# Turning queries, keys, convolution inputs and attention probabilities without TensorE

## The chip, the core and the metric

The kernel runs on one core of a Trainium2 chip. The metric is the device time of one execution in microseconds, the median of several runs. TensorE (PE in the rows) does the matrix products, VectorE (DVE) and ScalarE (ACT) the elementwise work, SyncE (SP) does nothing but issue DMA transfers, and GpSimd (POOL) has a few constants and row loads. Each engine works through its own list of instructions in order; semaphores tie the lists together.

## What is computed

Three blocks over 256 tokens of width 2048, in fp32 throughout: a gated MLP block, a stick-breaking attention block of 16 heads, and a block with an mLSTM branch (4 heads of 256) and a softmax attention branch (8 heads of 128), followed by an MLP. The parts that the change touches:

```python
# stick-breaking attention, per block of 128 queries
z = jnp.einsum('bhqd,bhkd->bhqk', qblk, kh)
a = jnp.where(mask, jnp.exp(log_sigmoid(z) + tail), 0.0)
o = jnp.einsum('bhqk,bhkd->bhqd', a, vh)

# mLSTM queries and keys: causal depthwise convolution of width 4, then silu
up = jnp.pad(u, ((0, 0), (3, 0), (0, 0)))
out = b
for j in range(4):
    out = out + w[j] * up[:, j:j + S]

# softmax attention (one block of 256 keys), after rotary embedding
p = jax.nn.softmax(jnp.where(causal, q @ k.T * scale, -inf))
o = p @ v
```

A matrix product contracts over the partition axis. So queries and keys, which the projections give with tokens on the partitions, have to be turned to have the head's channels there, the probabilities have to be turned to have the keys there, and the convolution wants channels on the partitions and tokens along the free axis.

## The kernel before

Weights stream from memory once. They are cut into 914 **groups** of 512 KB. A group is loaded by one DMA into one of 5 slots of `t_stage` (`load_group`), then split by ScalarE into a high part `t_wh` (`split_group`, an ACTIVATE of 128x1024) and by VectorE into the rest `t_wl` (a TENSOR_TENSOR of 128x1024). TensorE then runs 12 matmuls of 128x512 on it in `proj`: low weights by high input, high by high, high by low, for two 128-row tiles of weights and two halves of the tokens. `AHEAD = 4`: before the matmuls of group j the split of group j+4 is written out, and that split may start only when TensorE has finished group j-1, since there are 5 slots of split weights too. `load_group` waits for the split that frees its slot of `t_stage`.

Everything else is cut into **pieces**, which `later()` puts into one first-in, first-out list. After each group `offer()` may write out the next piece, if it has waited its number of groups (1 unless stated). So a piece's instructions stand on every engine between two groups, and their place in each engine's order is fixed when the program is built. `t_pool4` is a ring of four 4 KB-a-partition buffers (`temps`), `trans` two PSUM banks for transposes, `misc` two for small products.

What the change touches, before:

- `heads_t` (L906) turns a chunk of four heads of queries or keys in two pieces. Each takes 4 TensorE transposes against the identity (a **set** below) into a PSUM bank, and one ScalarE copy to `qt`, `kt_` in `t_vreg`. It is called 8 times in the stick-breaking block and 4 times in the softmax branch.
- `turn` (L949) turns a 128x512 tile of probabilities by one set and one ScalarE copy; three units in each of 4 chunks of the stick-breaking block and of 2 chunks of the softmax branch. In the stick-breaking block `four` calls it and `five` uses its result in `weighted`; in the softmax branch `two` and `three` do.
- `conv_t` (L1210) turns two heads of 128 channels at a time by a set, ScalarE copies them into `pad` behind three zero columns, `taps` computes the 4 taps per head on VectorE, and `second` the silu. Four calls.
- `to_xt` (L552) is another way to turn, in use already for the inputs of the large products: VectorE transposes 32x32 blocks within their partitions (two STREAM_TRANSPOSE of 128x512), then four DMAs on SyncE's queue, one per quarter of the partitions, carry the blocks to their place. The reader waits for the four landings. At most four such transfers are under way (`s_turn`).

Of the kernel before, what the change touches and what calls it, by code (L numbers as in the profile page):

```python
# [179 lines left out]
def _program(nc, A, out, ctx):  # L180
# [30 lines left out]
    pad, _ = sb("pad", [128, 2, 260], offset=s_at + 4096)  # L211
# [339 lines left out]

    def to_xt(src, marks, c, xh, xl, ready, gain=None, scale=1.0, done=None, wait=1):  # L552
# [3 lines left out]
        def send():  # L556
            zn, z, free = temps.take()
            quadrants = xl[:, 4 * c:4 * c + 4, :].bitcast(F32).rearrange("p k (i a s) -> p a (k i) s", i=2, a=4)
            zv = z.rearrange("p x y -> p (x y)")
            blocks = zv.rearrange("p (b k i s) -> p b k i s", b=4, k=4, i=2)  # L560
            for i in range(2):
                turned = DV.do(lambda e, i=i: e.block_transpose(
                    blocks[:, :, :, i], src(i).rearrange("p (k r b) -> p b k r", k=4, b=4)), *marks, *free)
            if done is not None:
                done(turned)
            n = turn_count[0]
            turn_count[0] += 1
            s_ = s_turn[n % 4]
            before = ((s_, 64 * (n // 4)),) if n >= 4 else ()
            for a in range(4):  # L570
                landed = SP.dma(lambda e, a=a: e.dma_start(
                    quadrants[:, a], zv[32 * a:32 * a + 32, :]),
                    s_, 64 * (n // 4) + 64, turned, *before)
            temps.give(zn, landed)
            st["landed"] = landed
# [337 lines left out]
    def heads_t(src, mark, dst, marks, done, wait=1):  # L913

        for b in range(2):
            def piece(b=b):
                x, m = src(), mark()
                n, t, free = trans.take()
                for j in range(2):
                    for i in range(2):  # L920
                        f = lambda e, j=j, i=i: e.transpose(t[:, 256 * j + 128 * i:256 * j + 128 * i + 128],
                                                            x[:, i, 128 * (2 * b + j):128 * (2 * b + j) + 128],
                                                            ident)
                        if i == 1 and j == 1:
                            tp = PE.do(f)
                        else:
                            PE.run(f, m, *free)
                a = AC.do(lambda e: e.activation(dst[:, 2 * b:2 * b + 2, :], t.rearrange("p (h s) -> p h s", h=2),
                                                 ACT.Copy), tp)
                trans.give(n, a)  # L930
                marks.append(a)
                if b == 1:
                    done(tp)
            later((piece, wait if b == 0 else 1))

    def scores(q, k, i, heads, marks):

        nk = 128 * (i + 1)
        n, t, free = misc.take()
        for j, h in enumerate(heads):  # L940
            f = lambda e, j=j, h=h: e.matmul(t[:, nk * j:nk * j + nk], q[:, h, 128 * i:128 * i + 128],
                                             k[:, h, 0:nk], start=True, stop=True)
            if j == len(heads) - 1:
                mm = PE.do(f)
            else:
                PE.run(f, *marks, *free)
        return n, t.rearrange("p (h k) -> p h k", k=nk), mm

    def turn(src, dst, mark):  # L949

        n, t, free = trans.take()
        for b in range(4):
            f = lambda e, b=b: e.transpose(t[:, 128 * b:128 * b + 128], src[:, 128 * b:128 * b + 128], ident)
            if b == 3:
                tp = PE.do(f)
            else:
                PE.run(f, mark, *free)
        a = AC.do(lambda e: e.activation(dst, t, ACT.Copy), tp)
        trans.give(n, a)
        return a  # L960
# [17 lines left out]
    def sb_unit(c, i, heads, qk_marks, v_view, v_mark, finish):  # L978
# [33 lines left out]
        def five():  # L1012
            n, t, mm = weighted(st["r"], v_view, i, heads, st["a"], v_mark)
# [193 lines left out]
    pad_free = [()]  # L1207
    pad_mark = DV.do(lambda e: e.memset(pad[:, :, 0:3], 0.0), *h_marks[3])

    def conv_t(src, mark, dst, base, marks, done):  # L1210

        def taps(j, b, s):
            ch = base + 2 * b + j
            x = s["t"][:, 0, 256 * j:256 * j + 256]
            m = DV.do(lambda e: e.tensor_scalar(x, pad[:, j, 0:256], cw[:, ch:ch + 1], gc[:, 80 + ch:81 + ch],
                                                ALU.mult, ALU.add), s["a"], *s["free"])
            for w in range(1, 4):
# [5 lines left out]
        for b in range(2):  # L1223
            s = {}

            def first(b=b, s=s):
                n, t, free = trans.take()
                for j in range(2):
                    for i in range(2):
                        f = lambda e, j=j, i=i: e.transpose(t[:, 256 * j + 128 * i:256 * j + 128 * i + 128],  # L1230
                                                            src[:, i, 128 * (2 * b + j):128 * (2 * b + j) + 128],
                                                            ident)
                        if i == 1 and j == 1:
                            tp = PE.do(f)
                        else:
                            PE.run(f, mark, *free)
                a = AC.do(lambda e: e.activation(pad[:, :, 3:259], t.rearrange("p (h s) -> p h s", h=2), ACT.Copy),
                          tp, pad_mark, *pad_free[0])
                trans.give(n, a)
                s["n"], s["t"], s["free"] = temps.take()  # L1240
                s["a"] = a
                taps(0, b, s)
                if b == 1:
                    done(tp)

            def second(b=b, s=s):
                m = taps(1, b, s)
                x, th = s["t"][:, 0, :], s["t"][:, 1, :]
                pad_free[0] = (m,)
# [5 lines left out]
            later((first, 2), second)  # L1255
# [207 lines left out]
    def soft_unit(c, u, i, heads, q, k, v, qk_marks, v_mark, ha, finish):  # L1463
# [25 lines left out]
        def three():  # L1489
            n, t, mm = weighted(st["r"], v, i, heads, st["t"], v_mark)  # L1490
# [12 lines left out]
    def soft_chunk(c):  # L1503
# [32 lines left out]
        later(u0[0], u1[0], u0[1], u0[2], u1[1], u2[0], u1[2], (u2[1], 2), u2[2])  # L1536
# [243 lines left out]
```

How the kernel before makes its waits and increments, by code:

```python
    def wait(self, *marks):  # L87
        for sem, value in marks:
            if self.seen.get(sem.name, 0) < value:
                self.seen[sem.name] = value
                self.items.append(lambda e, s=sem, v=value: e.wait_ge(s, v))
# [1 line left out]
    def do(self, emit, *marks):  # L93
        self.wait(*marks)
        self.n += 1
        f = emit(BOUND)
        self.items.append(lambda e: f(e).then_inc(self.sem, 1))
        return (self.sem, self.n)
# [5 lines left out]
    def dma(self, emit, sem, value, *marks):  # L105
        self.wait(*marks)
        f = emit(BOUND)
        self.items.append(lambda e: f(e).then_inc(sem, 16))
        return (sem, value)
```

## Time and profile before

| | us |
|---|---|
| median of 3 runs (2634.42 to 2636.94) | 2636.9 |
| the profiled execution, its own time | 2635.97 |
| its span in the profile | 2634.2 |
| TensorE busy | 2614.1 (99%) |
| VectorE busy | 1603.1 (61%) |
| ScalarE busy | 1218.5 (46%) |
| chain that ended last | TensorE 95% |

TensorE has hardly any idle time. Its matmuls are pipelined: one of 128x512 has a duration of about 390 ns in the rows, but the next starts 227 ns later, so cost is read from starts and not from durations. The blocks in time: gated MLP up to about 756 us, stick-breaking attention to about 1115, its output product to about 1205, the mLSTM projections and gates to about 1465, the softmax branch to about 1610, and then products to the end.

### The profile page before, as it was taken

To read this page: it belongs to the slowest core of one execution; us is meant where nothing else is said; L and a number is where in the kernel's file an instruction comes from. 1 tells how busy PE (TensorE), PEld (TensorE's weight loads), DVE (VectorE), ACT (ScalarE), POOL (GpSimd) and SP (SyncE) were. 2 spreads that over 40 slices of the span, in tenths; PEclk is the share of its full clock that TensorE was granted. 3 is DMA by queue.
4 is the path that set the end of the run, shared out by engine and by line. 5 is a ranking of instruction groups with operands and counts; after the bars stand their busy time and mean duration, and the time that the engine had idled before them with its cause. 6 is when DMAs were issued, how large, how long until landed. Compare 5 with 4: busy or idle time off the path is not lost.

```text
span 2634.2 us, 29949 instructions
## 1 busy us (share of the span) xinstructions
PE 2614.1 (99%) x11775; PEld 2162.1 (82%) x11775; DVE 1603.1 (61%) x1852; ACT 1218.5 (46%) x1478; POOL 20.8 (1%) x46
## 2 busy tenths in 40 slices
PE   9999999999999999999999999999999999999999
PEld 7888888888888888887888888888878888888887
DVE  5546665566657666766866666555576565565564
ACT  6554443444454444455444444444454344344443
POOL 1000000000000000000000000000000000000000
PEclk9999999999999999999999999999999999999999
DMA  7666666676765555677565666666657566676773
GB/s 250 192 193 202 204 197 201 193 211 197 216 203 173 171 166 167 191 226 222 160 179 173 183 185 184 200 200 200 219 172 224 192 204 214 189 217 207 199 223 130
DMA packets 437997, 515.39 MB, mean 196 GB/s; under 512 B 198480, under 2 KB 200640, under 8 KB 437856
## 3 DMA queue, kind: packets, MB, share of 16 engines
q1 hardware_dynamic: 435328, 506.29, 63.4%
q0 software_dynamic: 2384, 6.93, 1.1%
q8 instruction: 92, 1.51, 0.2%
q14 instruction: 49, 0.40, 0.0%
q10 hardware_dynamic: 144, 0.26, 0.0%
HBM read 488.24 MB, written 2.10 MB: 186 GB/s over the span
## 4 chain that ended last, share of the span: by engine, by line
PE 95%; DVE 2%; DMA 1%; ACT 1%; issue 1%; SPq 1%; DVEq 0%; ACTq 0%
PE bank L33 94%; PE bank L36 1%; DVE t_wl L51 1%; SPq L72 1%; DMA t_ytl<-t_pool 0%; DMA t_stage<-in_a_w_in_dram 0%; ACT t_wh L42 0%; DVE t_pool L39 0%; DVE t_pool L51 0%; ACT t_pool L42 0%; ACT t_yth L42 0%; DMA t_xtl<-t_pool 0%; ACT t_xth L42 0%; DVE t_pool L54 0%; DVE t_hres L51 0%
## 5 line engine op out<-in xcount | busy, mean ns | idle before, releaser
L51 DVE TENSOR_TENSOR t_wl<-t_stage,t_wh 128x1024 fp32r<-128x1024 f32 x914 | 1101.9, 1220 | 686.1 <-ACT t_wh L42 684.3
L42 ACT ACTIVATE t_wh<-t_stage 128x1024 fp32r<-128x1024 f32 x914 | 953.2, 1056 | 823.2 <-PE bank L33 809.5
L33 PE MATMUL bank<-t_wl,t_xth 128*128 128x512 f32 x2496 | 987.0, 395 | 9.4 <-DVE t_wl L51 7.0
L33 PE MATMUL bank<-t_wh,t_xtl 128*128 128x512 f32 x2496 | 973.8, 390 | 0.0
L33 PE MATMUL bank<-t_wh,t_xth 128*128 128x512 f32 x2496 | 972.4, 390 | 0.2 <-ACT t_wh L42 0.2
L33 PEld LDWEIGHTS bank<-t_wl,t_xth 128*128 128x128 f32 x2496 | 469.4, 188 | 106.5 <-DVE t_wl L51 9.3
L33 PEld LDWEIGHTS bank<-t_wh,t_xtl 128*128 128x128 f32 x2496 | 469.1, 188 | 99.8 <-DVE t_wl L51 0.5
L33 PEld LDWEIGHTS bank<-t_wh,t_xth 128*128 128x128 f32 x2496 | 469.6, 188 | 95.1 <-ACT t_wh L42 0.6
L33 PE MATMUL bank<-t_wl,t_yth 128*128 128x512 f32 x1024 | 399.2, 390 | 0.0
L33 PE MATMUL bank<-t_wh,t_ytl 128*128 128x512 f32 x1024 | 398.4, 389 | 0.0
L33 PE MATMUL bank<-t_wh,t_yth 128*128 128x512 f32 x1024 | 398.3, 389 | 0.0
L33 PEld LDWEIGHTS bank<-t_wl,t_yth 128*128 128x128 f32 x1024 | 192.2, 188 | 40.4 <-DVE t_ytl L54 0.3
L33 PEld LDWEIGHTS bank<-t_wh,t_yth 128*128 128x128 f32 x1024 | 192.2, 188 | 40.1 <-issue 0.2
L33 PEld LDWEIGHTS bank<-t_wh,t_ytl 128*128 128x128 f32 x1024 | 192.2, 188 | 39.8
L54 DVE SCALAR_TENSOR_TENSOR t_ytl<-t_ytl,t_yth 128x1024 fp32r<-128x1024 f32 x32 | 39.2, 1225 | 127.8 <-ACT t_yth L42 127.8
L42 ACT ACTIVATE t_pool<-bank,t_scl 128x512 f32<-128x512 f32 x120 | 75.9, 684 | 82.2 <-PE bank L33 77.0
L42 ACT ACTIVATE t_yth<-t_ytl 128x1024 fp32r<-128x1024 f32 x32 | 33.9, 1061 | 147.0 <-DMA t_ytl<-t_pool 147.0
L39 DVE STREAM_TRANSPOSE t_pool<-t_pool 128x512 f32<-128x512 f32 x72 | 74.2, 1069 | 0.0
L51 DVE TENSOR_TENSOR t_pool<-t_pool 128x1024 f32<-128x1024 f32 (+2 forms) x48 | 39.3, 819 | 25.1 <-ACT t_pool L42 23.3
L42 ACT ACTIVATE t_vreg<-bank 128x512 f32<-128x512 f32 (+1 forms) x39 | 21.6, 555 | 69.4 <-PE bank L36 42.2
L33 PE MATMUL bank<-t_wl,t_mth 128*128 128x512 f32 x128 | 49.8, 389 | 0.0
L33 PE MATMUL bank<-t_wh,t_mth 128*128 128x512 f32 x128 | 49.8, 389 | 0.0
(195 smaller groups left out, 978.6 us busy)
## 6 DMA issues: line engine op xcount, KB each, us to landing
t_stage<-in_a_w_in_dram SPq DMA_DIRECT2D x192, 512.0 KB, 4.4
t_stage<-in_w_in_dram SPq DMA_DIRECT2D x178, 512.0 KB, 4.2
t_stage<-in_b_w_in_dram SPq DMA_DIRECT2D x128, 512.0 KB, 3.7
t_stage<-in_w_up_dram SPq DMA_DIRECT2D x128, 512.0 KB, 3.9
t_stage<-in_w_down_dram SPq DMA_DIRECT2D x128, 512.0 KB, 4.2
t_stage<-in_a_w_out_dram SPq DMA_DIRECT2D x64, 512.0 KB, 4.2
t_ytl<-t_pool SPq DMA_DIRECT2D x128, 128.0 KB, 3.2
t_stage<-in_b_w_out_dram SPq DMA_DIRECT2D x32, 512.0 KB, 5.3
```

Of the source, the lines that this page charges most:

```text
L33: return lambda e: e.matmul(*a, **k)
L36: return lambda e: e.transpose(*a, **k)
L39: return lambda e: e.transpose(out, in_)
L42: return lambda e: e.activation(*a, **k)
L51: return lambda e: e.tensor_tensor(*a, **k)
L54: return lambda e: e.scalar_tensor_tensor(*a, **k)
L72: return lambda e: e.dma_start(*a, **k)
```

## The change

`send_turned` and `turn_chunk` are the two halves of `to_xt`, made functions of their own. `heads_t` becomes one piece: two STREAM_TRANSPOSE and four DMAs into the query or key buffer; it takes one more buffer of the ring, and its DMAs wait also for the last scores that read the buffer. `turn` becomes one STREAM_TRANSPOSE of 128x512 from `e` to `r` and four DMAs of half the bytes back into `e`. `conv_t` turns all four heads at once in a piece `send`, into a second ring buffer, and computes the taps two groups later from there; a tap that looks back by n tokens reads and writes ranges shifted by n, so `pad` and its zeros are gone. In `soft_chunk` the second unit's turn now stands before the first unit's weighted sum, and the last weighted sum waits two groups.

```diff
     def heads_t(src, mark, dst, marks, done, wait=1):
-        for b in range(2):
-            def piece(b=b):
...
-                a = AC.do(lambda e: e.activation(dst[:, 2 * b:2 * b + 2, :], t.rearrange("p (h s) -> p h s", h=2),
-                                                 ACT.Copy), tp)
...
-            later((piece, wait if b == 0 else 1))
+        def piece():
+            x = src()
+            n, z, free = temps.take()
+            zv = z.rearrange("p x y -> p (x y)")
+            turned = turn_chunk(lambda i: x[:, i, :], zv, (mark(), *free))
+            done(turned)
+            landed = send_turned(zv, dst.rearrange("p h (i a s) -> p a (h i) s", i=2, a=4), turned, *scored)
+            temps.give(n, landed)
+            marks.append(landed)
+        later((piece, wait))
...
+    def turn(src, via, mark):
+        turned = DV.do(lambda e: e.block_transpose(
+            via.rearrange("p (b c s) -> p b c s", b=4, c=4), src.rearrange("p (c r b) -> p b c r", c=4, b=4)), mark)
+        return send_turned(via, src.rearrange("p (c a s) -> p a c s", c=4, a=4), turned)
...
+    def send_turned(flat, rows, turned, *marks):
+        n = turn_count[0]
+        turn_count[0] += 1
+        s_ = s_turn[n % 4]
+        before = ((s_, 64 * (n // 4)),) if n >= 4 else ()
+        for a in range(4):
+            landed = SP.dma(lambda e, a=a: e.dma_start(rows[:, a], flat[32 * a:32 * a + 32, :]),
+                            s_, 64 * (n // 4) + 64, turned, *before, *marks)
+        return landed
...
-                m = DV.do(lambda e: e.scalar_tensor_tensor(
-                    out=x, in0=pad[:, j, w:w + 256], scalar=cw[:, 16 * w + ch:16 * w + ch + 1], in1=x,
-                    op0=ALU.mult, op1=ALU.add), m)
+                m = DV.do(lambda e: e.scalar_tensor_tensor(
+                    out=y[:, back:256], in0=x[:, 0:256 - back],
+                    scalar=cw[:, 48 - 16 * back + ch:49 - 16 * back + ch], in1=y[:, back:256],
+                    op0=ALU.mult, op1=ALU.add), m)
...
+        later((send, 2), (f0, 2), s0, f1, s1_)
...
-        later(u0[0], u1[0], u0[1], u0[2], u1[1], u2[0], u1[2], (u2[1], 2), u2[2])
+        later(u0[0], u1[0], u0[1], u1[1], u0[2], u2[0], u1[2], (u2[1], 2), (u2[2], 2))
```

The change moves instructions on the queues. Three places, each before and after. First, SyncE's list through the first chunk and a half of the stick-breaking block (`t_stage<-in_b_w_in_dram` is a weight load, `t_pool_61` the ring, `t_vreg` the query or key buffer).

```order
L72 DMA t_stage<-in_b_w_in_dram 128x2x512 [waits dve] x113
```

```order
L72 DMA t_stage<-in_b_w_in_dram 128x2x512 [waits dve] x12
L72 DMA t_pool_61<-t_pool_61 128x4x32 [waits turn2,dve]
L72 DMA t_pool_61<-t_pool_61 128x4x32 x3
L72 DMA t_stage<-in_b_w_in_dram 128x2x512 [waits dve] x5
L72 DMA t_pool_61<-t_pool_61 128x4x32 [waits turn3,dve]
L72 DMA t_pool_61<-t_pool_61 128x4x32 x3
L72 DMA t_stage<-in_b_w_in_dram 128x2x512 [waits dve] x5
```

Where only weights were loaded, each unit now puts four small transfers between two loads; twelve weight loads after the keys comes the first, and five loads lie between the units.

Second, VectorE's list at the first convolution (`t_gsm`, `t_dt`: the gates' last piece; `t_cw`: tap weights).

```order
L51 TENSOR_TENSOR t_dt<-t_dt,t_tri 128x1024 [waits act]
L51 TENSOR_TENSOR t_wl<-t_stage,t_wh 128x1024 [waits pe,act] x2
L48 TENSOR_SCALAR t_pool_61<-t_pad,t_cw,t_gc 128x256 [waits dve,act]
L54 SCALAR_TENSOR_TENSOR t_pool_61<-t_pad,t_cw,t_pool_61 128x256 [waits dve] x3
L51 TENSOR_TENSOR t_wl<-t_stage,t_wh 128x1024 [waits pe,act]
L48 TENSOR_SCALAR t_pool_61<-t_pad,t_cw,t_gc 128x256
```

```order
L51 TENSOR_TENSOR t_dt<-t_dt,t_tri 128x1024 [waits act]
L51 TENSOR_TENSOR t_wl<-t_stage,t_wh 128x1024 [waits pe,act] x2
L39 STREAM_TRANSPOSE t_pool_61<-t_pool_61 128x16x32 [waits dve]
L39 STREAM_TRANSPOSE t_pool_61<-t_pool_61 128x16x32
L51 TENSOR_TENSOR t_wl<-t_stage,t_wh 128x1024 [waits pe,act] x2
L48 TENSOR_SCALAR t_pool_61<-t_pool_61,t_cw,t_gc 128x256 [waits turn0]
```

The first tap waited for a ScalarE copy; now it waits for the transfer (`turn0`), two splits after the transposes. The four pieces of taps then follow in four consecutive groups, where they had three groups for two.

Third, VectorE's list in the softmax branch, from the end of the keys' rotary embedding to the first unit's mask (`t_neg`).

```order
L51 TENSOR_TENSOR t_pool_61<-t_pool_61 128x4x64 [waits dve]
L51 TENSOR_TENSOR t_wl<-t_stage,t_wh 128x1024 [waits pe,act] x5
L51 TENSOR_TENSOR t_pool_61<-bank,t_neg 128x512 [waits dve,pool,pe]
```

```order
L51 TENSOR_TENSOR t_pool_61<-t_pool_61 128x4x64 [waits dve]
L51 TENSOR_TENSOR t_wl<-t_stage,t_wh 128x1024 [waits pe,act] x3
L39 STREAM_TRANSPOSE t_pool_61<-t_pool_61 128x16x32 [waits dve]
L39 STREAM_TRANSPOSE t_pool_61<-t_pool_61 128x16x32
L51 TENSOR_TENSOR t_wl<-t_stage,t_wh 128x1024 [waits pe,act]
L51 TENSOR_TENSOR t_pool_61<-bank,t_neg 128x512 [waits turn2,pool,pe]
```

The keys' transposes stand one split ahead of the first unit, so on TensorE one group of matmuls lies between that place and the scores that read the keys.

## Rows read from the trace of the kernel before

**Rows 1.** The page: busy time of each engine.
```profile
PE 2614.1 (99%) x11775; PEld 2162.1 (82%) x11775; DVE 1603.1 (61%) x1852; ACT 1218.5 (46%) x1478; POOL 20.8 (1%) x46
```
**Rows 2.** Groups by line: count, busy us, mean ns, idle before and releaser.
```profile
L36 PE MATMUL bank<-t_ident,t_pool 128*128 128x128 f32 x200 | 29.9, 272 | 1.5 <-DVE t_pool L51 1.5
```
**Rows 3.** TensorE's timeline (start us, us) at the first queries, stick-breaking block.
```profile
753.71 0.39 PE L33 MATMUL bank<-t_wl,t_xth 128*128 128x512 f32 x1
...
756.44 0.60 PE L36 MATMUL bank<-t_ident,t_pool 128*128 128x128 f32 x4
...
759.65 0.60 PE L36 MATMUL bank<-t_ident,t_pool 128*128 128x128 f32 x4
```
**Rows 4.** Critical chain at two turns by DMA; the DMA issues of a small load.
```profile
1078.38 1.06 DVE t_pool L39
...
1082.35 3.21 DMA t_ytl<-t_pool
...
1088.95 2.08 DVE t_pool L39 x2
...
1093.23 3.11 DMA t_ytl<-t_pool
```
```profile
t_vreg<-in_norm_g_dram SPq DMA_DIRECT2D x1, 16.0 KB, 1.6
```
**Rows 5.** VectorE's and TensorE's timelines at stick-breaking units: split, then weighted sum.
```profile
815.16 1.22 DVE L51 TENSOR_TENSOR t_wl<-t_stage,t_wh 128x1024 fp32r<-128x1024 f32 x1
...
829.63 1.22 DVE L51 TENSOR_TENSOR t_wl<-t_stage,t_wh 128x1024 fp32r<-128x1024 f32 x1
...
1054.34 2.35 DVE L51 TENSOR_TENSOR t_wl<-t_stage,t_wh 128x1024 fp32r<-128x1024 f32 x2
...
1066.47 1.22 DVE L51 TENSOR_TENSOR t_wl<-t_stage,t_wh 128x1024 fp32r<-128x1024 f32 x1 [0.17 <-ACT t_wh L42]
```
```profile
820.52 1.05 PE L33 MATMUL bank<-t_vreg,t_pool 128*128 128x128 f32 x8
...
836.41 1.05 PE L33 MATMUL bank<-t_vreg,t_pool 128*128 128x128 f32 x8
...
1058.77 1.05 PE L33 MATMUL bank<-t_vreg,t_pool 128*128 128x128 f32 x8
...
1073.75 1.05 PE L33 MATMUL bank<-t_vreg,t_pool 128*128 128x128 f32 x8
```
**Rows 6.** Timelines of VectorE, ScalarE and TensorE in the first convolution.
```profile
1277.26 2.35 DVE L51 TENSOR_TENSOR t_wl<-t_stage,t_wh 128x1024 fp32r<-128x1024 f32 x2
...
1279.97 1.52 DVE L54 SCALAR_TENSOR_TENSOR t_pool<-t_pad,t_cw,t_pool 128x256 f32<-128x256 f32 x3
...
1285.21 0.69 DVE L54 SCALAR_TENSOR_TENSOR t_vreg<-t_pool 128x512 f32<-128x512 f32 x1 [0.70 <-ACT t_pool L42]
```
```profile
1287.46 1.26 ACT L42 ACTIVATE t_vreg<-bank,t_scl 128x512 f32<-128x512 f32 x2
```
```profile
1294.93 0.39 PE L33 MATMUL bank<-t_wl,t_xth 128*128 128x512 f32 x1
```
**Rows 7.** Timelines of VectorE and TensorE in the softmax branch, first chunk.
```profile
1474.57 4.62 DVE L51 TENSOR_TENSOR t_wl<-t_stage,t_wh 128x1024 fp32r<-128x1024 f32 x4
...
1481.33 0.42 DVE L51 TENSOR_TENSOR t_pool<-t_pool,t_cosb 128x256 f32<-128x256 f32 x1
...
1508.70 1.23 DVE L51 TENSOR_TENSOR t_wl<-t_stage,t_wh 128x1024 fp32r<-128x1024 f32 x1 [0.79 <-ACT t_wh L42]
```
```profile
1470.29 0.39 PE L33 MATMUL bank<-t_wl,t_xth 128*128 128x512 f32 x1
...
1498.46 1.05 PE L33 MATMUL bank<-t_vreg 128*128 128x128 f32 x8
```
**Rows 8.** Start of the program: a window with its granted clock, and the chain.
```profile
16.00:20.00 4.00, 3.45 (x8) 2.77 (x9) 3.20 (x6) 1.64 (x3) 0.00 (x0) 0.50 1.02 394
```
```profile
16.55 5.49 PE bank L33 x12
```

More of the change, by code:

```diff
@@ L559, in send @@
             zv = z.rearrange("p x y -> p (x y)")
[L560 to L563, printed above, removed]
+            turned = turn_chunk(src, zv, (*marks, *free))
             if done is not None:
                 done(turned)
[L566 to L573, printed above, removed]
+            landed = send_turned(zv, quadrants, turned)
             temps.give(zn, landed)
@@ L913, in heads_t @@
     def heads_t(src, mark, dst, marks, done, wait=1):
[L915 to L934 removed]
+        def piece():
[8 more added lines that the diff above has]
+        later((piece, wait))
+    scored = []
     def scores(q, k, i, heads, marks):
@@ L946, in scores @@
                 PE.run(f, *marks, *free)
+        scored.append(mm)
         return n, t.rearrange("p (h k) -> p h k", k=nk), mm
[L949 to L960, printed above, removed]
+    def turn(src, via, mark):
+        turned = DV.do(lambda e: e.block_transpose(
+            via.rearrange("p (b c s) -> p b c s", b=4, c=4), src.rearrange("p (c r b) -> p b c r", c=4, b=4)), mark)
+        return send_turned(via, src.rearrange("p (c a s) -> p a c s", c=4, a=4), turned)
     def weighted(at_, v, i, heads, *marks):
@@ L1204, in gates_five @@
         temps.give(gate["n2"], gate["dt"])
[L1207 to L1208 removed]
     def conv_t(src, mark, dst, base, marks, done):
[L1212 to L1217, printed above, removed]
+        st = {}
@@ new lines, in send, with taps @@
+        def send():
+            n, z, free = temps.take()
+            zv = z.rearrange("p x y -> p (x y)")
+            turned = turn_chunk(lambda i: src[:, i, :], zv, (mark, *free))
+            done(turned)
+            st["n"], x, free = temps.take()
+            st["x"] = x.rearrange("p x y -> p (x y)").rearrange("p (h s) -> p h s", h=4)
+            st["a"] = send_turned(zv, st["x"].rearrange("p h (i a s) -> p a (h i) s", i=2, a=4), turned, *free)
+            temps.give(n, st["a"])
+        def taps(h, y, marks_):
+            ch = base + h
+            x = st["x"][:, h, :]
+            m = DV.do(lambda e: e.tensor_scalar(y, x, cw[:, 48 + ch:49 + ch], gc[:, 80 + ch:81 + ch],
+                                                ALU.mult, ALU.add), st["a"], *marks_)
+            for back in range(1, 4):
@@ L1218, in taps, with smooth @@
                 m = DV.do(lambda e: e.scalar_tensor_tensor(
-                    out=x, in0=pad[:, j, w:w + 256], scalar=cw[:, 16 * w + ch:16 * w + ch + 1], in1=x,
+                    out=y[:, back:256], in0=x[:, 0:256 - back],
+                    scalar=cw[:, 48 - 16 * back + ch:49 - 16 * back + ch], in1=y[:, back:256],
                     op0=ALU.mult, op1=ALU.add), m)
             return m
-        for b in range(2):
+        def smooth(b):
             s = {}
[L1226 to L1242, printed above, removed]
-                if b == 1:
[L1244 to L1249, printed above, removed]
@@ L1250, in second, with first @@
+            def first():
+                s["n"], s["t"], free = temps.take()
+                taps(2 * b, s["t"][:, 0, 0:256], free)
+            def second():
+                m = taps(2 * b + 1, s["t"][:, 0, 256:512], ())
+                x, th = s["t"][:, 0, :], s["t"][:, 1, :]
+                if b == 1:
+                    temps.give(st["n"], m)
                 a = AC.do(lambda e: e.activation(th, x, ACT.Tanh, scale=0.5), m)
@@ L1254, in second @@
                 marks.append(v)
-            later((first, 2), second)
+            return first, second
+        (f0, s0), (f1, s1_) = smooth(0), smooth(1)
+        later((send, 2), (f0, 2), s0, f1, s1_)
     ym_ready = {}
```

11 lines of the change are left out of this document (8 added, 3 removed).

## The prediction

> **What bounds the kernel now.** I read the page first: TensorE is busy 99% of the span [rows 1]. Then the groups by line, for what the change removes: 200 transposes, and one wait of 1.5 us before them [rows 2]. So nothing gains by a lighter ScalarE or VectorE; only instructions taken off TensorE's list, or waits on it, change the end. Then I read timelines side by side, for the question that decides: when does TensorE ask for a turned tile, and when would it have landed?
>
> **What is removed.** A mean duration of 272 ns says little, since transposes overlap. Without a set a group takes 756.44 - 753.71 = 2.73 us; with a set it takes 759.65 - 756.44 = 3.21 us [rows 3]. A set costs 0.48 us. The sets are 16 + 8 of `heads_t`, 12 + 6 of `turn`, 8 of `conv_t`: 50, so 24.0 us. The one wait was for the rotary embedding before the first query set of the softmax branch; with no set there, 1.5 us more go. ScalarE's copies go too and are worth nothing. Removed: **25.5 us**.
>
> **What a turn costs by the new way.** The same mechanism is at work in `to_xt`. From the end of the second STREAM_TRANSPOSE to the last landing: 1091.03 to 1096.34 is 5.3 us; where splits run back to back beside it, 1079.44 to 1085.56 is 6.1 us [rows 4]. Of it 2.2 us are three issues before the last, and 3.1 to 3.2 the last transfer. The transposes take 2.1 us for a chunk, 1.07 for a tile of probabilities. The half-size transfer of `turn` is not in the trace. A transfer of its 128-byte blocks with all bytes takes 3.1, one of 16 KB takes 1.6 [rows 4]; between them lies 2.3, and with about 2.0 for the issues I take L = 4.3, with 3.1 and 6.1 as the ends.
>
> The Trainium skill ("SBUF — State Buffer", on the DMA setup-cost knee) says that a transfer pays a fixed cost of some 2 us that doesn't scale with bytes. By that a half-size turn would save almost nothing against a full one, L would be 5.3 and the stick-breaking stalls below 21.5 us in place of 10.3. No row here shows the half size.
>
> **Stick-breaking block.** The order is unchanged but for the turns. In the first unit VectorE ends the split ahead of the turn at 816.38, the turn at 817.45, so the tile lands at 821.75. TensorE wants it at 820.52, less the 0.48 of the set that stood between, 820.04: it stalls 1.7 us (L - 2.6). Second unit: 830.85 + 1.07 + 4.3 = 836.2 against 835.9, 0.3 us (L - 4.0); in the last chunk the gate's work holds VectorE back to 1055.56, and it is 1060.9 against 1058.3, 2.6 us. Third unit: 1067.69 + 1.07 + 4.3 = 1073.1 against 1073.3, none [rows 5]. Four chunks: 4 x 1.7 + 3 x 0.3 + 2.6 = **10.3 us** (3.4 at L = 3.1, 31 at 6.1). Queries and keys have groups to spare there: at least six between the keys' turn and the scores, 16 us against a landing of 5 to 6. SyncE's weight loads stand behind the four turn issues, 2.9 us; a load is issued five groups, 13.6 us, ahead of its split, so that is covered.
>
> **Convolutions.** Here VectorE is the engine that waits, and everything behind the taps on its list waits with it, the splits first. Its pieces: a split 1.14, taps of a head 1.9, ScalarE's tanh 0.7, the product 0.7 [rows 6]. Before, three groups held three splits, two heads' taps, a tanh and a product with 0.3 us of a wait for ScalarE, 3.4 + 3.8 + 0.7 + 0.7 + 0.3 = 8.9 us, against TensorE's 3 x 2.72 + 0.48 = 8.6: nothing was to spare. Now: the split of group 442 ends at 1279.5, the transposes at 1281.6, the landing is at 1287.7. After two more splits VectorE is at 1284.0 and stands still for 3.7 us. Taps to 1289.6, split 445 to 1290.9, second taps, tanh and product to 1294.1; ScalarE meanwhile does tanh, then two evacuations of 1.26 [rows 6], then its half of split 446, and VectorE's half ends at 1296.9. TensorE wants group 446 at 1294.93 less three sets, 1293.5: it stalls 3.6 us. Going on by the same durations I get 0.4, 2.1, 1.5 and 2.1 us at the next groups, and 5.0 us where the first mLSTM head needs the last key product, which now ends three groups before it, not five. That is 14.7 us; the second chunk, whose head comes later, gives 7.5 by the same working. With 5.3 us in place of 6.1 for the landings both together give 19.3. I take **20.8 us** (12 to 27; the low end is for landings that let VectorE catch up once).
>
> **Softmax branch.** Queries have time, keys have not. In the first chunk VectorE is behind already: it ends the split of group 506 at 1478.06 (third of four), the queries' transposes at 1480.1, then split, rotary (6 operations, 2.4 us), split, rotary, three splits: 1490.8; the keys' transposes to 1492.9, landing at 1498.2. TensorE starts group 502 at 1470.29 and wants the keys seven groups of 2.72 later, at 1489.3 [rows 7]: a stall of 8.9 us. In the second chunk VectorE is not behind, its split ends 0.14 us before TensorE's group does (1067.69 plus two groups and a set is 0.14 short of 1073.75 [rows 5]); so -0.14 + 2.07 + 5.3 - 2.72 = 4.5 us. First unit: from the scores to the end of the split ahead of the turn is 1509.93 - 1498.46 = 11.5 us, since masks, maxima and exponentials of both units stand there [rows 7]; with 1.07 + 4.3 the tile lands 16.9 us after the scores. TensorE has two scores (1.6) and four groups (10.9) until then, 12.5: a stall of 4.4 us in each chunk. The second unit is covered by that stall, the third by its two groups. Together 8.9 + 4.5 + 8.8 = **22.2 us** (14 to 27).
>
> **Clock.** At the program's start TensorE stood idle some 4 us, its granted clock then read 0.50 of full, the lower of its two levels (1.2 GHz), and a group of 12 took 5.49 us instead of 2.77 [rows 8]. I count this once, behind the 8.9 us stall, **2.7 us**; stalls of 4 to 5 us may each do it too, up to 13.5 in all.
>
> **Sum.** -25.5 + 10.3 + 20.8 + 22.2 + 2.7 = +30.5 us. On the profiled execution's own 2635.97 that is 2666.5; the median of the runs shown is 0.9 higher, so 2667.
>
> **Rivals.**
> - *The transfers are hidden* (the side of faster). The price is the removed 25.5 us: 2611. It decides at a landing within 2.6 us of the transpose for the first stick-breaking units and 2.7 + 0.14 - 2.07 = 0.8 us for keys. Against it stand the 5.3 and 6.1 of the same mechanism [rows 4]; for it, that 16 KB land in 1.6, and that TensorE's gaps are short of my places by a group or so in each case, which one misread place could undo. Chance 0.12, for anything under 2631.6.
> - *Convolutions cost little.* If VectorE and ScalarE catch up between the calls and only the two attentions stall: -25.5 + 32.5 + 2.7 = +9.7, with a small L less: 2638 to 2647. For it: the mLSTM pieces behind them give TensorE long groups. Against: before, the product of rows 6 stood at every third group without idle time to spare. Chance 0.15, of which 0.10 is within 0.2%.
> - *The stalls run on.* Full-size latency for the half-size turn, the clock falling at each stall of 4 us: +11.2 + 10.8 on top, 2689, and up to 2700 with late weight loads. Chance 0.10.
> - *A transpose is worth its duration.* If each of the 200 gave back 0.272 us [rows 2] the removal would be 54 us and the sum +0.5 us: 2637. Starts contradict it: 3.21 against 2.73 [rows 3]. Chance 0.02, in the "within" part. The Trainium skill ("TensorE: Matmul & The Clock Gate", Part 4) gives about 275 ns for such a transpose in a kernel, so reading its figure as a price leads here; the trace agrees with the duration and not with the price.
> - *That the change doesn't do what it says*: its order shows all 50 sets gone, so no chance is kept for it.
>
> **Numbers.** Forecast as summed, 2647 to 2690: 0.61. The range from 2636 to 2692 leaves out the faster case and the upper tail. A measurement here can tell about 0.2%, 5.3 us, from no change. Faster 0.12; within 0.12; slower 0.76.
>
> **What would show it.** TensorE's waits should name DMA `t_vreg<-t_pool` (keys, 8.9 and 4.5 us) and DMA `t_pool<-t_pool` (12 + 6 weighted sums, the first units longest); VectorE should wait for DMA `t_pool<-t_pool` before four first taps, 3 to 4 us each, and TensorE for VectorE's `t_wl` from about 1290 to 1320 us. The set count must be 0 in `t_pool`. The forecast is wrong if those waits are absent, if the landings of the half size come in 3 us, or if TensorE's list in the convolutions has no waits for `t_wl`.

## The result, and the profile after

The changed kernel takes 2687.6 us (median of 4 runs, 2682.9 to 2688.6) against 2636.1 before (4 runs, the three shown and one more): a ratio of 1.0195, 95% interval 1.0183 to 1.0207. It is 51.6 us slower. The forecast was 2667, so the sign and the mechanisms were right and the size was 21 us short; the range of 2647 to 2690 held the result with 2.4 us to spare.

The page, where TensorE was busy 99% [rows 1], now reads:

```profile
span 2685.9 us, 29800 instructions
...
PE 2615.2 (97%) x11575; PEld 2153.8 (80%) x11575; DVE 1650.7 (61%) x1901; ACT 1193.9 (44%) x1428; POOL 20.9 (1%) x46
...
PE 77%; DVE 10%; DMA 4%; SPq 3%; issue 3%; ACT 3%; DVEq 0%; ACTq 0%
```

The 200 transposes [rows 2] are gone from TensorE's count (11775 to 11575), and of the chain that ended last TensorE holds 77% where it held 95%. What TensorE waits for (line, us in total, times, longest), over the whole span, then VectorE's waits in the convolutions:

```profile
PE bank L33 <- DMA t_pool<-t_pool: 22.3, 14, 3.7
PE bank L33 <- DVE t_wl L51: 18.2, 16, 2.9
PE bank L33 <- DMA t_vreg<-t_pool: 14.5, 2, 9.0
PE bank L33 <- DVE t_vreg L54: 4.7, 2, 4.5
```
```profile
DVE t_pool L48 <- DMA t_pool<-t_pool: 15.7, 4, 4.2
```

They are the three kinds that the prediction named: turned probabilities (22.3 us), splits that come late (18.2 over the whole span, 11.6 of it from 1280 to 1465 us, the convolutions; before there were 8.5, none of it there), and the softmax keys (14.5). Where the time came in is read from the starts of TensorE's groups in the timelines of both traces:

| groups, us from start to start | before | after | difference |
|---|---|---|---|
| 0 to 2, program's start | 22.3 | 18.9 | -3.4 |
| 2 to 262, gated MLP | 726.0 | 726.0 | 0.0 |
| 262 to 371, stick-breaking | 331.8 | 338.5 | +6.7 |
| 371 to 437 | 188.9 | 189.7 | +0.8 |
| 437 to 487, convolutions, mLSTM | 152.5 | 175.1 | +22.6 |
| 487 to 548, softmax branch | 194.1 | 219.2 | +25.1 |
| 548 to 912 | 1002.3 | 1002.2 | -0.1 |

The first row belongs to no part of the change: of the twelve kernels traced here eight ran their first group at a lower clock, as in [rows 8], and four did not. From group 2 on the change costs 55.1 us. Each row is one execution, and a block repeats only so well: the stick-breaking block, 338.5 us here, took 337.1, 339.1 and 342.3 us in three kernels below that leave it as it is (conv_late, undo_keys, undo_conv), with one to three stretches at a lower clock in it.

**A first unit of the stick-breaking block.** The chain of waits (start, us, what), then TensorE's timeline at its end:

```profile
811.06 1.08 DVE t_pool L39
812.14 0.02 issue
812.16 0.62 SPq L72
...
814.17 2.65 DMA t_pool<-t_pool
```
```profile
814.47 0.39 PE L33 MATMUL bank<-t_wh,t_xtl 128*128 128x512 f32 x1
816.86 1.16 PE L33 MATMUL bank<-t_vreg,t_pool 128*128 128x128 f32 x8 [2.00 <-DMA t_pool<-t_pool]
817.77 0.48 PE L33 MATMUL bank<-t_wl,t_xth 128*128 128x512 f32 x1
```

The transpose ends at 812.14 and the last of four transfers lands at 816.82: 4.7 us, where 4.3 was assumed. TensorE would have started at 814.47 + 0.23 and starts at 816.86, 2.2 us late (forecast 1.7). It also restarts slowly: 0.91 us to the next matmul, where the same eight without a wait took 0.81 before (820.52 [rows 5] to 821.33).

**The first convolution.** VectorE's timeline:

```profile
1283.67 2.07 DVE L39 STREAM_TRANSPOSE t_pool<-t_pool 128x512 f32<-128x512 f32 x2
1285.67 2.31 DVE L51 TENSOR_TENSOR t_wl<-t_stage,t_wh 128x1024 fp32r<-128x1024 f32 x2
1292.17 0.41 DVE L48 TENSOR_SCALAR t_pool<-t_pool,t_cw,t_gc 128x256 f32<-128x256 f32 x1 [4.19 <-DMA t_pool<-t_pool]
...
1299.95 1.23 DVE L51 TENSOR_TENSOR t_wl<-t_stage,t_wh 128x1024 fp32r<-128x1024 f32 x1 [1.40 <-ACT t_wh L42]
```

Against [rows 6] this is the forecast chain: two splits, then VectorE stands 4.19 us (forecast 3.7), and the split that TensorE wants next ends at 1301.2. TensorE starts that group 3.0 us late (forecast 3.6).

**The softmax keys.** TensorE's timeline at the first scores of each chunk, then two windows (us, busy time and count of PE, PEld, DVE, ACT, POOL, granted clock, share of DMA, GB/s):

```profile
1526.60 2.05 PE L33 MATMUL bank<-t_vreg 128*128 128x128 f32 x8 [9.04 <-DMA t_vreg<-t_pool]
1528.31 0.77 PE L33 MATMUL bank<-t_wl,t_xth 128*128 128x512 f32 x1
...
1612.32 2.05 PE L33 MATMUL bank<-t_vreg 128*128 128x128 f32 x8 [5.42 <-DMA t_vreg<-t_pool]
```
```profile
1061.00:1066.00 5.00, 5.00 (x20) 4.09 (x20) 2.77 (x6) 1.33 (x2) 0.00 (x0) 0.66 0.60 195
...
1544.00:1552.00 8.00, 7.29 (x25) 6.24 (x26) 2.26 (x5) 0.00 (x0) 0.00 (x0) 0.62 0.94 228
...
1612.00:1620.00 8.00, 7.68 (x26) 6.51 (x27) 2.99 (x6) 2.60 (x9) 0.00 (x0) 0.60 0.15 55
```

From start to start the stalls are 9.2 and 5.6 us (forecast 8.9 and 4.5). The windows show what was counted once: behind the stalls the granted clock falls to its lower level, 0.50 of full or 1.2 GHz, for part of the window, and matmuls start 0.43 us apart instead of 0.23. There are nine such stretches between 890 and 1640 us, each behind a wait of 2.5 us or more; the waits of 2.2 us or less in this trace had none behind them. Their matmuls of 128x512 cost 13.0 us more than at full clock, and scores and weighted sums some 3 us more.

### The profile page after: what moved, and what is told of

Read it like the earlier page. It is cut to its first block, busy times and chain, and to the rows that moved or that the text cites. A ratio compares the mean times of both kernels' runs of the same rounds, so it can differ in the third digit from the quotient of the medians.

```text
span 2685.9 us, 29800 instructions
## 1 busy us (share of the span) xinstructions
PE 2615.2 (97%) x11575; PEld 2153.8 (80%) x11575; DVE 1650.7 (61%) x1901; ACT 1193.9 (44%) x1428; POOL 20.9 (1%) x46
## 4 chain that ended last, share of the span: by engine, by line
PE 77%; DVE 10%; DMA 4%; SPq 3%; issue 3%; ACT 3%; DVEq 0%; ACTq 0%
PE bank L33 77%; DVE t_wl L51 4%; SPq L72 3%; DMA t_pool<-t_pool 2%; DVE t_pool L39 2%; DVE t_pool L54 1%; ACT t_wh L42 1%; DMA t_ytl<-t_pool 1%; DVE t_pool L51 1%; ACT t_pool L42 1%; DVE t_pool L63 0%; DMA t_xtl<-t_pool 0%; DVE t_pool L48 0%; DMA t_stage<-in_a_w_in_dram 0%; PE bank L36 0%
## 5 line engine op out<-in xcount | busy, mean ns | idle before, releaser
L33 PEld LDWEIGHTS bank<-t_wl,t_xth 128*128 128x128 f32 x2496 | 472.4, 189 | 124.7 <-DVE t_wl L51 24.6
L39 DVE STREAM_TRANSPOSE t_pool<-t_pool 128x512 f32<-128x512 f32 x122 | 126.9, 1074 | 0.0
L33 PE MATMUL bank<-t_wh,t_mtl 128*128 128x512 f32 x128 | 49.8, 389 | 0.0
```

Source lines behind the costliest of these rows:

```text
L33: return lambda e: e.matmul(*a, **k)
L39: return lambda e: e.transpose(out, in_)
```

## Experiments

Theory: the loss is latency against distance. Each turned tile or split comes later than TensorE wants it, by what the prediction's sums give, and the clock's price stands on top. Rivals: transfers are slow because they are crowded; VectorE's work is too dense; one stall only hides another. All ratios are to the kernel before on the same chip. Differences from 2687.6 us compare separate sets of runs, whose kernel before took 2636.1 us there and 2635.1 or 2634.5 below; taken over each set's kernel before, what is given back is 1.0 to 1.6 us less than stated below.

### One part undone

Three kernels put one part of the change back to TensorE and ScalarE.

> The changed kernel with the convolutions done as before: TensorE transposes, ScalarE copies into the padded tile, taps as before. Everything else as changed. Theory A (what the trace of the changed kernel says: the two chunks of convolutions add 26.3 us of stalls, slow clock and restarts to TensorE, and save 8 sets of 0.48): 2687.6 - 26.3 + 3.8 = 2665 us, with no wait of VectorE for a turned tile of the convolutions, and TensorE's waits for VectorE's low weights down from 18 us to the 8 or 9 of the kernel before. Theory B (the prediction's sizes, 20.8 us of stalls and no clock in it): 2687.6 - 20.8 + 3.8 = 2670.6 us. Theory C (VectorE's backlog in the convolutions was only shifted from elsewhere, so undoing it frees less): 2675 us or more.

> The changed kernel with the tiles of probabilities turned as before, by TensorE and ScalarE, in both attentions, and the units of the softmax branch in their old order. Queries, keys and convolutions as changed. Theory A (the trace: stick-breaking block 20.2 us of stalls, restarts and slow clock less 5.8 us for 12 sets; softmax branch 9.2 us of waits before weighted sums, 0.7 of restarts, 4.3 of slow clock, less 2.9 for 6 sets): 2687.6 - 14.4 - 11.3 = 2662 us. Theory B (the prediction's sizes, 10.3 and 8.8 us of stalls): 2687.6 - 4.5 - 5.9 = 2677 us. Theory C (the waits before the weighted sums are partly VectorE's delay from the convolutions and keys, which stays): between the two, with TensorE still waiting over 3 us before some weighted sum.

> The changed kernel with the keys of the softmax branch turned as before, by TensorE and ScalarE; its queries and all the rest as changed. Theory A (the trace: waits for the keys of 9.2 and 5.6 us, the slow clock behind them some 4.5 us, less 1.9 us for 4 sets): 2687.6 - 17.4 = 2670 us, no wait of TensorE for a transfer into the key buffer. Theory B (the prediction's sizes, 13.4 us of stalls and 2.7 of clock): 2687.6 - 14.2 = 2673 us. Theory C (the stall for the keys hid VectorE's backlog; without it the first unit's weighted sum waits longer by as much): 2680 us or more, and the wait before the first weighted sum of the branch grows from 3.7 to 8 us or more.

The edits in their cores, in the same order: `conv_t` with its `pad`, `turn` with the order of the softmax units, and `heads_t` for the softmax keys, each as in the kernel before (`heads_pe` is its `heads_t`):

```diff
-        later((send, 2), (f0, 2), s0, f1, s1_)
...
+            later((first, 2), second)
```
```diff
-        return send_turned(via, src.rearrange("p (c a s) -> p a c s", c=4, a=4), turned)
...
+        a = AC.do(lambda e: e.activation(dst, t, ACT.Copy), tp)
...
-        later(u0[0], u1[0], u0[1], u1[1], u0[2], u2[0], u1[2], (u2[1], 2), (u2[2], 2))
+        later(u0[0], u1[0], u0[1], u0[2], u1[1], u2[0], u1[2], (u2[1], 2), u2[2])
```
```diff
-            heads_t(lambda r=r: r["t"], lambda r=r: r["m"], dst, qk_marks,
+            (heads_t if part == 0 else heads_pe)(lambda r=r: r["t"], lambda r=r: r["m"], dst, qk_marks,
```

| undone | us | ratio (95%) | given back | trace said | prediction's sizes |
|---|---|---|---|---|---|
| convolutions | 2664.5 | 1.0110 (1.0095 to 1.0126) | 23.1 | 22.5 | 17.0 |
| probabilities | 2664.9 | 1.0117 (1.0103 to 1.0131) | 22.7 | 25.7 | 10.4 |
| softmax keys | 2672.3 | 1.0144 (1.0130 to 1.0158) | 15.3 | 17.4 | 14.2 |

Theory A holds for the convolutions and, 3 us short, for the probabilities. For the keys 15.3 us lies between A and B and tells them not apart; what falls is theory C. The parts hardly hide one another: 23.1 + 22.7 + 15.3 = 61.1 us, and the turned queries and keys that stay give 10.8 back (below), which leaves 50 of the 51.6 (47 when each is taken over the kernel before of its own set). Without the stall for the keys, TensorE's waits in the softmax branch are

```profile
PE bank L33 <- DMA t_pool<-t_pool: 8.9, 3, 4.1
```

where they were 8.5 us in four beside 14.5 for the keys. The wait for the first weighted sum did not grow to 8 us, so the keys' stall had hidden no backlog of VectorE.

### One part alone

> The kernel before with one part of the change: the queries and keys of the stick-breaking block and the queries of the softmax branch are turned by VectorE and transfers; keys of the softmax branch, probabilities and convolutions stay with TensorE. 20 sets of 0.48 us and the old wait of 1.5 us go. Theory A (these turns have the groups to spare that their latency of 5.4 to 8 us needs): 2636.1 - 9.6 - 1.5 = 2625 us, a ratio of 0.9958. Theory B (2.1 us more of VectorE's time per chunk and four more issues ahead of the weight loads push splits late): 2630 to 2640 us, with new waits of TensorE for the low weights near 860, 935, 1010 or 1480 us.

It is the changed kernel with all three edits above at once.

2624.3 us, ratio 0.9960 (0.9947 to 0.9972): 10.8 us faster than before on that chip. A set is worth 0.48 us when nothing waits for its substitute; the stick-breaking block took 324.1 us from group 262 to 371 in place of 331.8, 7.7 for 16 sets. This is the part that was right to change.

### More distance: the weighted sums one group later

> The changed kernel with the weighted sums of the three stick-breaking units one group later: three groups of matmuls in place of two between a turn and its reader, by another order of the pieces alone. In the trace of the changed kernel the waits before these twelve sums are 15.6 us from start to start, the restarts some 2.1, two half-clock stretches 2.6. Theory A (it is latency against distance: a half-size turn lands 4.4 to 5.4 us after its transpose and two groups minus VectorE's work are too short for it, three are enough): only 0.6 to 0.9 us of wait before the second unit of the last chunk stay, and the time is 2687.6 - 19.5 = 2668 us. Theory B (the transfers are late because weight loads and splits crowd them, so landings move with their place): waits of 1 us or more stay before several of the sums, 2675 us or more.

```diff
-        later(u0[0], u0[1], u0[2], u1[0], u0[3], u1[1], u0[4], u1[2], u2[0], u1[3], u2[1], u1[4], u2[2],
-              (u2[3], 2), (u2[4], 2))
+        later(u0[0], u0[1], u0[2], u1[0], u0[3], u1[1], u1[2], u0[4], u2[0], u1[3], u2[1], u2[2], u1[4],
+              (u2[3], 2), (u2[4], 3))
```

2669.6 us, ratio 1.0135 (1.0121 to 1.0149). Between 750 and 1080 us TensorE has no wait left at all, where the changed kernel has

```profile
PE bank L33 <- DMA t_pool<-t_pool: 13.7, 10, 3.2
```

and groups 262 to 371 take 318.5 us in place of 338.5, 20.0 less; the median is 18.0 less (forecast 19.5). Part of the 20.0 goes again right behind the block: groups 371 to 437 take 191.7 us in place of 189.7, with a wait of 2.2 us for VectorE and a granted clock of 0.63 from 1104 to 1108 us, where the changed kernel had a wait of the same length and no lower clock. Landings are no earlier than they were, 4.4 to 5.5 us behind the transpose. So it was distance.

### More distance for the convolutions

> The changed kernel with the first taps of each convolution call four groups after the transposes in place of two, nothing else; the pieces behind move by two groups for each call. Theory A (what costs there is that VectorE stands still up to 4.2 us for the landing, with splits queued behind it): VectorE's waits for a turned tile of a convolution (15.7 us in four) vanish, TensorE's waits for low weights near 1296 to 1327 and 1406 to 1434 us fall from about 11 us to under 3, and the time is some 12 to 18 us lower, 2670 to 2675 us. Theory B (it is the density: transposes and four tap pieces in a row are more work for VectorE than the groups they lie in, 2.1 + 4 x 1.15 + 4 x 1.9 + 4 x 0.7 = 17.1 us against 5 x 2.72 = 13.6): VectorE's waits vanish but TensorE's stay within a third of what they were, 2683 us or more.

```diff
-        later((send, 2), (f0, 2), s0, f1, s1_)
+        later((send, 2), (f0, 4), s0, f1, s1_)
```

2663.9 us, ratio 1.0116 (1.0103 to 1.0130), 23.7 us less: more than either theory gave. VectorE's and TensorE's waits there (1270 to 1440 and 1270 to 1465 us), then TensorE's from 1495 to 1680:

```profile
DVE t_pool L48 <- DMA t_pool<-t_pool: 3.6, 3, 1.4
```
```profile
PE bank L33 <- ACT t_pool L42: 0.3, 1, 0.3
```
```profile
PE bank L33 <- DVE t_ytl L54: 3.4, 1, 3.4
```

The four pieces of taps still stand in four consecutive groups and TensorE waits for no split, so theory B falls: the loss was VectorE standing with splits behind it. The two more groups also give VectorE some time between transposes and taps; this run does not separate the two. The price comes at the end. The pieces behind move by up to five groups, the product that reads the softmax branch waits 3.4 us for its input, and groups 548 to 912 take 1009.9 us in place of 1002.2; the last weighted sum now stands among them too.

### Idle time filled with matmuls

> The changed kernel with idle time filled: before each of 24 waits at which TensorE stood still in the attentions and convolutions it runs as many matmuls of 128x512 on the inputs, into a free PSUM bank that nobody reads, as fit at 0.227 us into the gap that the trace of the changed kernel shows there (1 to 40, 247 in all, 56 us). They add nothing to the result. In the trace of the changed kernel nine stretches of half clock follow such gaps; the 128x512 matmuls in them cost 13.0 us more than at full clock, the scores and weighted sums some 2 us more. Theory A (the stalls themselves bring the clock down, and its cost stands on top of them): the granted clock stays at 1.00 through 750 to 1670 us, and 13 to 15 us come back: 2673 to 2675 us. Theory B (the clock's price is partly absorbed: TensorE, being slower, meets the next tile or split later, and at full clock it would only have waited): the clock stays up, but less than 8 us come back, 2680 us or more. Theory C (the clock falls for another reason): half-clock stretches stay, 2687 us or more.

```diff
+        n, t, free = trans.take()
+        PE.wait(*free)
+        for b in range(count):
+            f = lambda e: e.matmul(t, tokens(xth, 0, 0), xth[:, 0:2, :].rearrange("p k s -> p (k s)"),
+                                   start=True, stop=True)
```

(The counts add up to 237, 54 us; the expectation says 247.) The same windows as above, and TensorE's timeline at the first keys:

```profile
1061.00:1066.00 5.00, 5.00 (x28) 4.21 (x27) 3.13 (x4) 1.33 (x2) 0.00 (x0) 1.00 0.82 211
...
1544.00:1552.00 8.00, 8.00 (x41) 6.76 (x40) 3.92 (x9) 2.79 (x7) 0.00 (x0) 1.00 0.74 189
1612.00:1620.00 8.00, 8.00 (x37) 6.60 (x36) 3.46 (x9) 4.94 (x15) 0.00 (x0) 1.00 0.24 66
```
```profile
1516.11 9.23 PE L33 MATMUL bank<-t_xth 128*128 128x512 f32 x40
1525.57 1.13 PE L33 MATMUL bank<-t_vreg 128*128 128x128 f32 x8 [0.23 <-DMA t_vreg<-t_pool]
1526.45 0.48 PE L33 MATMUL bank<-t_wl,t_xth 128*128 128x512 f32 x1
```

The clock stays at 1.00 wherever the idle time was filled. It falls once from 750 to 1670 us, to 0.58 from 1120 to 1124, behind a wait of 3.0 us for a split that was not on the list. So theory C falls: idle TensorE is what brings it down. The time is 2683.0 us, ratio 1.0187 (1.0173 to 1.0201); by medians that cannot be told from 1.0195, and as a time it is what theory B gave. The traces tell more, once the start is left out: from group 2 to 912 it takes 2642.8 us in place of 2650.8, 8.0 less. By stage the filling gives back 3.1 us in the stick-breaking block, 5.5 in the softmax branch and only 1.1 in the convolutions, where half clock had cost 4.2. There TensorE waits for VectorE's splits at one group after another, and a group that runs faster only waits longer at the next: 72 added matmuls of 0.227 us, 16.3 us, and still

```profile
PE bank L33 <- DVE t_wl L51: 3.9, 4, 1.4
```

make 20 us, against 16.3 us of waits there (from 1280 to 1465 us) in the changed kernel. So theory A describes the attentions and theory B the convolutions. By these two traces the clock's real price is about 8 us, not 13 to 16; the medians, 4.6 us apart, do not fix it better.

### Fewer issues in a row

> The changed kernel with the four transfers of each turned tile of probabilities issued by two engines, two on SyncE's queue and two on ScalarE's, in place of four on SyncE's; nothing else. Theory A (half of the latency is the issues: in the trace of the changed kernel the first three of four issues take 2.0 us of the 4.4 to 5.4 from the transpose's end to the landing): the landing comes some 1.3 us earlier, 3.3 to 4 us after the transpose; waits before first units of the stick-breaking block fall from 2.2 to about 1, most others there vanish, and with fewer half-clock stretches the time is 12 to 17 us lower, 2671 to 2675 us. Theory B (the data's own way takes the time, and issues only overlap with it): landings stay above 4.4 us and the time within 4 us of 2687.6. Theory C (ScalarE, waiting for the transpose and issuing for 1.3 us, delays its splits): landings earlier, but TensorE waits more for low weights, 2680 us or more.

```diff
-            landed = SP.dma(lambda e, a=a: e.dma_start(rows[:, a], flat[32 * a:32 * a + 32, :]),
+            landed = (queues or (SP,) * 4)[a].dma(lambda e, a=a: e.dma_start(rows[:, a], flat[32 * a:32 * a + 32, :]),
...
-        return send_turned(via, src.rearrange("p (c a s) -> p a c s", c=4, a=4), turned)
+        return send_turned(via, src.rearrange("p (c a s) -> p a c s", c=4, a=4), turned, queues=(SP, AC, SP, AC))
```

2692.6 us, ratio 1.0217 (1.0203 to 1.0231): no better, and by the median 5 us worse, though the two intervals overlap. The issues (issuer, count, KB each, median us to landing), first of the changed kernel, then of this one, and the first unit's chain:

```profile
t_pool<-t_pool SPq DMA_DIRECT2D x72, 64.0 KB, 2.8
```
```profile
t_pool<-t_pool SPq DMA_DIRECT2D x36, 64.0 KB, 3.2
t_pool<-t_pool ACTq DMA_DIRECT2D x36, 64.0 KB, 3.6
```
```profile
812.96 1.09 DVE t_pool L39
...
814.08 0.75 ACTq L72
...
814.86 0.80 ACTq L72
...
815.76 1.07 ACT t_wh L42
```

In the stick-breaking block of the changed kernel the four are issued 0.7 us apart, and land at medians of 0.5, 0.5 and 0.65 us behind one another. Here the last is issued at 0.7 behind the transpose in place of 2.0, and still lands 4.2 to 5.2 behind it: the first three land some 0.3 apart, and the last a median of 1.1 behind them. Theory A falls, and B holds for the landing, which the spacing of the issues does not set. Of theory C the chain shows the first half, ScalarE's split behind its two issues and VectorE's half behind that. The second half is missing: TensorE waits for no split in that block. It waits 18.1 us for turned tiles there, against 13.7 in the changed kernel and 16.0 in undo_conv, whose block is the changed kernel's; the block takes 343.1, 338.5 and 342.3 us in the three. So a loss by the second queue is not shown either.

### Versions meant to be faster

> A version meant to beat both kernels: queries and keys of the stick-breaking block, queries of the softmax branch and the probabilities of the stick-breaking block turned by VectorE and transfers, with those weighted sums one group later; convolutions, softmax keys and softmax probabilities by TensorE as before. 32 sets go. Theory A (with three groups between a turn and its reader the turns are free): heads_only's 2624.3 less 12 x 0.48 = 5.8 and plus 0.8 for the last chunk's second unit: 2619 us, a ratio of 0.994. Theory B (the waits before the weighted sums stay by half): 2626 us.

Against the kernel of heads_only, `turn` in the stick-breaking block is the changed one again (`turn_pe` is that of before, for the softmax units), with the order of units_late:

```diff
-            n, t, mm = weighted(st["r"], v_view, i, heads, st["a"], v_mark)
+            n, t, mm = weighted(st["e"], v_view, i, heads, st["a"], v_mark)
...
-            st["t"] = turn(st["e"], st["r"], st["a"])
+            st["t"] = turn_pe(st["e"], st["r"], st["a"])
```

2620.7 us, ratio 0.9951 (0.9938 to 0.9963): 13.8 us faster than before on that chip, by the median the best version here. Its page:

```profile
span 2618.7 us, 29871 instructions
...
PE 2600.9 (99%) x11647; PEld 2151.3 (82%) x11647; DVE 1633.2 (62%) x1884; ACT 1203.6 (46%) x1446; POOL 20.9 (1%) x46
```

TensorE is back at 99%. Groups 262 to 371 take 318.7 us, 13.1 less than before, for 28 sets of 0.48 = 13.4. Behind the block 1.9 us are lost again: groups 371 to 437 take 190.8 us in place of 188.9, with a granted clock of 0.77 and 0.81 from 1100 to 1108 us behind a wait of 2.3 us for a split. The medians of this and of heads_only lie 3.6 us apart with intervals that overlap, so that it is the better of the two rests on the block (318.7 against 324.1 us).

> The version that beat both kernels (stick-breaking queries, keys and probabilities and softmax queries by transfers, weighted sums one group later) with the convolutions by transfers as well, their first taps three groups after the transposes in place of the change's two. 8 more sets of 0.48 us go. Theory A (three groups cover nearly all of a landing of 6.1 to 6.4 us behind the transposes, VectorE waits 1.5 us at most per call): 2620.7 - 3.8 = 2617 us. Theory B (each call takes more groups of the list of pieces than before, so the mLSTM pieces and all of the softmax branch are written four or five groups later, and the turned sums of its last chunk come late for the product that reads them, as when the taps stood four groups behind, where 7.5 us were lost after group 548): no gain or a loss, 2620 to 2628 us.

Against the version above, the changed `conv_t` is back, with this edit:

```diff
-        later((send, 2), (f0, 2), s0, f1, s1_)
+        later((send, 2), (f0, 3), s0, f1, s1_)
```

2634.0 us, ratio 0.9996 (0.9987 to 1.0005): 13 us are lost again, more than theory B gave. TensorE's waits from 1230 to 1465 us, then to 1665:

```profile
PE bank L33 <- DVE t_vreg L54: 6.5, 2, 3.3
PE bank L33 <- DVE t_wl L51: 4.9, 3, 1.7
```
```profile
PE bank L33 <- ACT t_pool L42: 2.5, 2, 1.3
```

Three groups are not enough either: the key products come late for the mLSTM heads, splits come late behind VectorE's waits (11.1 us in four, over the whole span), and four pieces' delay is passed on. Groups 487 to 548 take 200.4 us in place of 190.7 in the version above, more than the 2.5 us of waits of the softmax branch, since work of the convolutions now lies among them. One of the two waits for key products ends there (3.25 us, up to 1416.00), with a granted clock of 0.57 from 1416 to 1420 us, and so does the work of one mLSTM head. By conv_late, where the same head has moved (146.3 us for groups 437 to 487, where 152.5 less 8 sets is 148.7), the head is worth an estimated 2.4 us.

## Why the prediction was right in sign and short in size

- **Removed, 25.5 us: right.** 16 sets alone gave back 7.7 us and 28 gave 13.1, 0.47 to 0.48 each. A transpose is not worth its 272 ns.
- **Stick-breaking stalls, 10.3 us: mis-sized, 15.6.** The step that failed is L = 4.3. The half-size turn took 4.4 to 5.4 us in this block, median 4.75 (4.6 to 7.5 in the softmax branch), since a half-size transfer took 2.8 us, nearer to the full size's 3.2 than to the 2.3 taken half way down. The sums were differences (L - 2.6, L - 4.0), so 0.45 us on L became 5 us, with 2.0 us at third units, counted at none. There the sum had the tile 0.2 us ahead of its reader (1073.1 against 1073.3), so any latency above its own brings a wait that it did not count. Restarts (some 1.4 us) and half clock (some 3) were on top; net the block is +6.7 us, where the sum had 10.3 - 13.4 = -3.1; by the other kernels with the same block, +5.3 to +10.5.
  The Trainium skill ("SBUF — State Buffer", on the DMA setup-cost knee) would have given, as an estimate by its fixed cost, L = 5.3 and 21.5 us of stalls. The trace agrees in kind, since half the bytes saved 0.4 us of 3.2, but not in amount: the truth lay half way between that estimate and the value taken.
- **Convolutions, 20.8 us: the chain and the stalls were right, the sum short.** VectorE's wait (4.19 against 3.7), the first stall (3.0 against 3.6, itself 0.2 above what its own numbers give, 1296.9 - 1293.5) and that of the mLSTM head (4.6 against 5.0) came as worked out, and all stalls of the stage together are 18.7 us from start to start. Net the stage is +22.6, and with 8 sets 26.4 were added. Of the 7.7 us beyond the stalls 4.2 are matmuls of 128x512 at half clock; the other 3.5, restarts and small matmuls at half clock among them, were not traced singly. Yet filling gave back only 1.1 us: at full clock most of that time would have been waiting for VectorE.
- **Softmax branch, 22.2 us: right to 2 us.** Keys 14.8 (13.4 forecast), first units 3.9 and 2.6 (4.4 each), third units 1.2 and 1.5 (none): 24.0. With 14 sets and the old wait (8.2) on top of the net 25.1, 33.3 were added; the 9 us beyond the stalls are half clock (6.2 in matmuls of 128x512), restarts and 1.1 us of late splits.
- **Clock, 2.7 us once: the step that failed.** The prediction held that stalls of 4 to 5 us may each do it and put the price at up to 13.5, and then took it once. It fell nine times, also behind waits of 2.5 and 3.4 us, for 13.0 us in matmuls of 128x512, of which about 8 count.
- **Sum.** Stage by stage: 9.8 (stick-breaking) + 5.6 (convolutions) + 8.4 (softmax, 25.1 against -8.2 + 22.2 + 2.7) + 0.8 between + 0.0 = 24.6, less 3.4 for the start, which was slower and at half clock in the profiled execution before and not in that after: 21.2, which is 51.7 - 30.5.

The rival "the stalls run on" said 2689 for full latency and the clock falling at each stall. Its time was nearer, and its second half was what happened; its first half was half true. That the stated range reached 2690 is owed to its width and not to the sum.

## To carry to other kernels

A turn that leaves TensorE for VectorE and transfers gives back 0.48 us per set and took 4.4 to 8 us to arrive here, so it pays exactly where the reader stands that far behind: count the groups between producer and reader first, and move the reader before moving the work. Where a wait sits on an engine that also prepares everybody's weights, what counts is what is queued behind it. When a sum is a difference between a latency and a distance, give the latency's error its full weight, and count the clock at every stall, not once.

## What the runs showed of the hardware

- In the changed kernel the granted clock fell behind a pause of TensorE of 2.7 us from start to start (888.39 to 891.09, then 0.79 over 888 to 896) and not behind one of 2.4 us (at 814.47, clock 1.00). The same unit of undo_conv had a pause of 2.3 us and there the clock fell (0.79 over 816 to 824), so the length of the pause alone does not decide it. With matmuls in the idle time it stayed at 1.00.
- Four transfers of 64 KB in 128-byte blocks, issued within 2.0 us by one engine or within 0.7 us by two, had all landed 4.4 to 5.4 and 4.2 to 5.2 us behind the transpose (stick-breaking block): faster issues did not bring the last landing forward.
- The first group ran at a lower clock in some executions and not in others: group 2 starts between 17.7 and 18.9 us in the four traces where the clock stayed at 1.00 and between 20.2 and 22.3 in the other eight. One profile of one kernel is uncertain by up to 4.6 us for its start alone.
